# Residual additions for two tiles at a time, and three weight splits moved into the gated linear attention's score sets

## The reference

```python
def second_block(x, norm_gains, ...):
    h = x.astype(jnp.float32)
    for layer in range(DEPTH_2):
        g = norm_gains[layer]
        y = rms_norm_2(h, g[0])
        y = sb_gla_mixer(y, ...) if layer % 2 == 0 else s5_mixer(y, ...)
        h = h + rms_norm_2(y, g[1])
        y = swiglu_ffn(rms_norm_2(h, g[2]), w_ffn_in[layer], w_ffn_out[layer])
        h = h + rms_norm_2(y, g[3])

def sb_gla_mixer(h, ...):
...
    o_gla = gla_chunked(q, k, v, log_a)            # gated linear attention, 8 heads
    o_gla = o_gla * lax.rsqrt(jnp.mean(o_gla * o_gla, axis=-1, keepdims=True) + NORM_EPS)
    o_gla = merge_heads(o_gla) * gla_norm_gain * jax.nn.silu(g_r)
    return jnp.concatenate([o_sb, o_gla], axis=-1) @ w_out
```

## Time and profile before

| | |
|---|---|
| median of 3 runs | 3559.05 us (3557.74 to 3559.19) |
| the profiled execution: its own time | 3562.0 us |
| its span | 3560.2 us |
| TensorE busy | 3471.8 us (98%) |
| VectorE busy | 2306.5 us (65%) |
| ScalarE busy | 1785.4 us (50%) |
| GpSimd busy | 490.5 us (14%) |

### The profile page before, as it was taken

One profiled execution on the slowest core, in us unless ns is written; L12 is line 12 of the kernel. 1 busy time (PEld: TensorE's weight loads), 2 busy tenths in 40 slices (PEclk: granted clock), 3 DMA queues, 4 the chain that ended last, 5 costly groups with the idle time before them and its releaser, 6 DMA issues.

```text
span 3560.2 us, 62732 instructions
## 1 busy us (share of the span) xinstructions
PE 3471.8 (98%) x21888; PEld 3027.7 (85%) x21888; DVE 2306.5 (65%) x3460; ACT 1785.4 (50%) x2735; POOL 490.5 (14%) x538
## 2 busy tenths in 40 slices
PE   9998999999999999999999999999699999999998
PEld 7886888888888888888888888887588888888887
DVE  5688565555555766675766677779755665565566
ACT  5477454545454554554555444444354554454453
POOL 0001410111114100123100001105012000000005
PEclk9999999999999999999999999999899999999999
DMA  6561545555555555443456556666235455555555
GB/s 212 170 188 56 189 152 193 183 192 185 190 187 189 170 188 174 162 154 127 150 193 196 186 188 195 203 224 227 58 118 186 148 192 190 186 187 192 184 188 189
DMA packets 190643, 626.70 MB, mean 176 GB/s; under 512 B 26822, under 2 KB 40200, under 8 KB 190360
## 3 DMA queue, kind: packets, MB, share of 16 engines
q1 hardware_dynamic: 179948, 612.48, 52.8%
q10 hardware_dynamic: 10572, 12.56, 1.2%
HBM read 620.52 MB, written 3.15 MB: 175 GB/s over the span
## 4 chain that ended last, share of the span: by engine, by line
PE 88%; DVE 7%; ACT 2%; DMA 1%; issue 1%; POOL 0%; SPq 0%; ACTq 0%; DVEq 0%; POOLq 0%
PE bank L1901 53%; PE bank L1904 28%; PE m L1924 1%; DVE w_lo L1045 1%; PE m L1914 1%; PE m L1926 1%; DVE prod L1713 1%; DMA w_raw<-stream 1%; DVE y L1072 0%; DVE st L1718 0%; DVE st L1716 0%; DVE w_lo L1049 0%; ACT w_hi L465 0%; DVE res L1078 0%; PE m L2394 0%
## 5 line engine op out<-in xcount | busy, mean ns | idle before, releaser
L1045 DVE TENSOR_TENSOR w_lo<-w_raw,w_hi 128x1024 fp32r<-128x1024 f32 x1086 | 1336.3, 1253 | 773.1 <-ACT w_hi L465 766.4
L1901 PE MATMUL bank<-act,w_hi 128*128 128x512 f32 x6016 | 1511.6, 393 | 3.7 <-DVE w_lo L1045 1.7
L465 ACT ACTIVATE w_hi<-w_raw 128x1024 fp32r<-128x1024 f32 x1090 | 1128.9, 1054 | 404.5 <-PE bank L1904 358.2
L1901 PEld LDWEIGHTS bank<-act,w_hi 128*128 128x128 f32 x6016 | 1082.5, 189 | 203.7 <-DVE w_lo L1045 4.4
L1904 PEld LDWEIGHTS bank<-act,w_lo 128*128 128x128 f32 x6016 | 820.8, 191 | 58.7
L1904 PE MATMUL bank<-act,w_lo 128*128 128x256 f32 x6016 | 838.9, 282 | 0.0
L1901 PE MATMUL bank<-ffn,w_hi 128*128 128x512 f32 x2432 | 613.6, 393 | 2.2 <-DVE w_lo L1049 1.8
L474 ACT ACTIVATE low<-bank 128x256 f32<-128x256 f32 x542 | 207.4, 383 | 749.7 <-PE bank L1904 748.7
L1901 PEld LDWEIGHTS bank<-ffn,w_hi 128*128 128x128 f32 x2432 | 436.5, 189 | 81.0 <-DVE w_lo L1049 3.2
L1904 PEld LDWEIGHTS bank<-ffn,w_lo 128*128 128x128 f32 x2432 | 334.0, 190 | 25.1
L1053 DVE TENSOR_TENSOR ev<-bank,low 128x256 f32<-128x256 f32 x468 | 197.9, 423 | 240.5 <-ACT low L474 236.9
(11 more groups left out here) (419 smaller groups left out, 2268.6 us busy)
## 6 DMA issues: line engine op xcount, KB each, us to landing
w_raw<-stream SPq DMA_DIRECT2D x1148, 512.0 KB, 3.4
b_part<-s_bt ACTq DMA_DIRECT2D x16, 256.0 KB
pow_b<-powers ACTq DMA_DIRECT2D x16, 256.0 KB
bias<-toeplitz SPq DMA_DIRECT2D x4, 512.0 KB, 8.7
out<-res SPq DMA_DIRECT2D x3, 512.0 KB, 2.8
res<-x_t SPq DMA_DIRECT2D x2, 512.0 KB, 8.8
res<-x_t ACTq DMA_DIRECT2D x2, 512.0 KB, 11.0
bias<-toeplitz SPq DMA_DIRECT2D x4, 256.0 KB, 11.8
```

The source lines that it names most:

```text
L465: a(w_hi[:, q, :], w_raw[:, q, :], ACT.Copy).then_inc(hi_ready, 1)
L1045: e.tensor_tensor(w_lo[:, q, :], w_raw[:, q, :], w_hi[:, q, :].bitcast(F32), ALU.subtract).then_inc(lo_ready, 1)
L1901: mm(bank[w][:, 0:2 * n], w_hi[:, q, wt], x(h * hk + k, 0, 2 * n), start=(h == 0 and k == 0), stop=False)
```

## The change

Two parts. In `add_residual` two tiles are added in one operation of 512 columns; the scale runs two tiles ahead, the add of a pair waits for both scales, and the low parts of the pair before follow behind it, two in a row. In the second mixer, the splits of halves 1 and 2 of `out2`'s first step are taken out of the last step of `in2` and, with that of half 3, put at part 4 of the first three head pairs (`it` = 4, 9, 14); the filling of `row_of` goes to `it == 4`.

```diff
@@ add_residual
             scale(0)
-            for k in range(DT):
-                if k + 1 < DT:
-                    scale(k + 1)
-                v.wait_ge(y_scaled, base + k + 1)
-                e.tensor_tensor(res[:, k, :], res[:, k, :], y[:, k, :], ALU.add).then_inc(res_added, 1)
+            scale(1)
+            for k in range(0, DT, 2):
+                if k + 2 < DT:
+                    scale(k + 2)
+                v.wait_ge(y_scaled, base + k + 2)
+                e.tensor_tensor(res[:, k:k + 2, :], res[:, k:k + 2, :], y[:, k:k + 2, :], ALU.add).then_inc(res_added, 2)
+                if k + 3 < DT:
+                    scale(k + 3)
                 if low_part and k >= 2:
                     low_part(k - 2)
+                    low_part(k - 1)
                 if between:
                     between(k)
+                    between(k + 1)
             if low_part:
                 low_part(DT - 2)
                 low_part(DT - 1)
@@ VectorE, second mixer
-            run_phase(v, "in2", lo, scaled_z, behind=sb_behind, skip=1, quiet=8, lone=lone_z)
+            
+            def in2_low(i, q):
+                if not (isinstance(i, int) and i == PH["out2"][0] and q):
+                    lo(i, q)
+            run_phase(v, "in2", in2_low, scaled_z, behind=sb_behind, skip=1, quiet=8, lone=lone_z)
             v.wait_ge(sem("masks_loaded"), 16)
-
-            e.tensor_copy(row_of[:, :, :], ident[0:2, 0:2].unsqueeze(2).to_broadcast([2, 2, P])).then_inc(sem("row_of"), 1)
...
-                if it == 14:
-                    lo(PH["out2"][0], 3)
+                if it == 4:
+                    e.tensor_copy(row_of[:, :, :], ident[0:2, 0:2].unsqueeze(2).to_broadcast([2, 2, P])).then_inc(sem("row_of"), 1)
+                if part == 4 and t < 3:
+                    lo(PH["out2"][0], t + 1)
```

## The result

The changed kernel takes 3566.09 us (median of 12 runs, 3562.99 to 3569.49), the kernel before 3559.12 (12 runs beside it, 3557.15 to 3562.98). The ratio is 1.0019 with an interval of 1.0011 to 1.0026: slower by 7.0 us, where +6.45 and 3565.5 were forecast. It lies just inside the bound of 0.2%.

A forecast was written before the change was run, and what follows sets the result against it. The prediction took TensorE, busy 98% of the span, as the bound, VectorE mattering only where TensorE waits. Part one +3.45 and part two +3.0 made +6.45 us on the median 3559.05: 3565.5, range 3561.0 to 3568.5.

The forecast's parts named there:

- The prices: VectorE instruction times at the stage entries: a double add 0.60 us instead of 0.68 for two single adds.
- The feed-forward entries: MLP and both feed-forwards: TensorE's first tile 0.96 us later, 0.9 more per entry, +2.7 for three.
- The gate's entry: Gated projection: ScalarE waits 0.33 us longer for the ninth add, the fourth weight split 0.15 more; +0.5.
- The S5 entry: Entry to the S5 stage: the first square follows three scales and a double add, so TensorE starts later; +0.65 us.
- The end: End of the program, VectorE on the path: eight pairs give back 0.6 us, net -0.4; the two last stores cost nothing.
- The first select and the first split: Gated linear attention: select starts 3.0 us earlier, fillers leave 0.7, copy and split before set 5 use it up; -0.1.
- The second split: Gated linear attention, ahead of set 10's selects, VectorE on the path: all of it added, +1.5 us.
- The clock: Set 12 in the gated linear attention: TensorE falls to half clock behind the longer wait; +1.6 us.
- VectorE as the bound: Rival at the entries: VectorE sets the pace, so grouping's 0.6 us per entry comes back; 3554.9 us, chance 0.10.
- the dear double add: Rival: a double add takes the 0.68 us of two and saves nothing; 3566.1 us, chance 0.05.
- The clock staying up: Rival: no clock fall behind set 12's longer wait, so 1.6 us less; 3563.9 us, chance 0.28.
- Falls at the entries: Rival: the clock also falls at feed-forward entries; 3567.1 us with one fall, 3570.3 with three; chance 0.17.

The follow-up runs named there:

- run 7: Kernel before with each low part one tile behind its addition instead of two, at the feed-forward and gate entries, additions single: 3557.97 us, ratio 0.9996.
- run 4: The change's moved splits and copy with single additions, but the second split behind set 7's selects, against the kernel before: 3559.59 us, ratio 1.0001.
- run 8: Kernel before with double additions in the last stage alone and the last two stores made one: 3558.54 us, ratio 0.9997.
- run 10: Splits of run 5, feed-forward low parts of run 7, end of run 8, and 8 filler matmuls instead of 24 ahead of set 2: 3554.50 us.
- run 6: Run 2 with 12 filler matmuls set into each of TensorE's waits before sets 12 and 17: 3560.29 us, ratio 1.0002 against the kernel before.
- run 11: The kernel before, unchanged, run again for a second trace: 3558.41 us, ratio 0.9997.
- run 1: The double additions alone, splits and copy as in the kernel before: 3564.85 us against 3559.5, ratio 1.0014.
- run 3: Kernel before with each stage's first four tiles added singly and the other twelve in pairs, splits as before: 3563.51 us, ratio 1.0012.
- run 5: Run 4 with the third split moved behind the loop, ahead of the last reciprocal: 3556.85 us against 3559.96 for the kernel before, ratio 0.9990.
- run 2: The moved splits and copy of the change alone, additions single as in the kernel before: 3563.26 us, ratio 1.0011.

## Why the prediction was right

- **The prices.** Double add 0.61 from start to start, taken as 0.60. Right.
- **The feed-forward entries.** First tile 0.99 later (0.96 forecast), each entry +0.87 (0.9). "What VectorE saves later has nobody waiting for it" holds: nothing came back. Run 7 shows the cause with the sign turned. The sentence on breaking instructions up in the Trainium skill, "Perfetto Trace Analysis", section "Optimizing Scalar/DVE Operations", says that where an engine isn't saturated but makes others wait, smaller instructions may let work finish sooner. The traces agree: on an engine at 65%, working in pairs made TensorE's idle time ahead of its first tile grow from 0.56 to 1.55. The size of the instruction is the small part of it: by the prediction's own prices 0.78 of the 0.96 are the two scales that the pairs draw ahead of the first low part, and 0.18 the adds.
- **The gate's entry.** +0.59, taken as 0.5. ScalarE's work behind the ninth add starts 0.38 later (1186.01, before 1185.64, from reciprocals 0.01 apart), forecast 0.33; the other 0.21 come behind it, where 0.15 was given to the fourth split. **The S5 entry.** From the first scale to the first square's sum +0.66, taken as 0.65; the other 1.0 in after is a fall of the clock that began ahead of the entry and that run 4 has with single additions.
- **The end.** Sized wrong: -0.05 instead of -0.4. The step that failed is "each is small, and I cost that at nothing": the issue of a store, 0.4, which used to hide beside the last addition, now stands behind it (run 8).
- **The first select and the first split.** Place right, sum too high: -0.1 was forecast, and from the reciprocal at 1286.68 to the first one inside the attention it is -0.88 (307.70 to 306.82). Of this 0.55 is the copy's price: I took 0.75 for it from its old place, and in the new one it takes 0.20 (1585.51 to 1585.71). The select before it was also done some 0.3 sooner than I had it. Run 10 shows that the fillers were what held set 2, as forecast.
- **The second split.** +1.5 forecast, 1.56 measured (run 6); run 4 removes it by moving that one split.
- **The clock.** +1.6 forecast behind set 12, 1.46 in the trace of after, and run 6 removes it with fillers. What I had wrong is that this was told as one certain event at one place. Falls come and go between executions of one kernel: after has one behind 2.19 us and none behind nearly the same wait at set 17, and the kernel before fell behind that wait in its first trace and not in its second (run 11). The two traces that were compared have two falls in the attention before and one after, so in them the attention is even 1.02 shorter with the change.
- **The sum.** Without falls the traces give 3 x 0.87 + 0.59 + 0.66 - 0.05 = +3.8 for part one and -0.88 + 1.56 = +0.7 for part two, together +4.5, where the forecast without its clock term was 4.85. The forecast then added one fall, 1.6. The measured +7.0 (by the interval, 3.9 to 9.3) leaves 2.5 for the clock, and the mean clock of the executions (run 6) gives about two more falls, 3.2 by that estimate. So the mechanism holds, but 6.45 came as near as it did by luck: the end was 0.35 too hopeful, the first select 0.8 too dear, and the clock was taken as one fall where it is nearer to two. Where the second one comes is open: the S5 entry of after has one, behind set 17's wait it has none, and one trace for each kernel can't give frequencies by place.
- **The rivals.** VectorE as the bound is out (run 7, and no gain behind the first tiles); the dear double add is out (0.61). The clock staying up holds in some executions at one of the two waits. Falls at the entries: none at the three feed-forward entries of after, in spite of 1.55 us without work. The falls near S5's entry (after, runs 1 and 4) and near ffn1's (runs 1, 3, 5 and 10) all began ahead of the first scale of their stage, from 0.4 us before to 1.0 behind its reciprocal, so the longer idle time ahead of the first tile did not bring them. The three kernels with double additions at the entries (after, runs 1 and 3) have five of the eight starred entries in the table; whether that is chance is not shown.

## What to carry to other kernels

Where VectorE feeds a saturated TensorE, count what stands ahead of the first output that the other engine waits for, and not the instructions in all: working in pairs moved that output 1.0 us back and saved nothing that anyone waited for, and taking one step out ahead of it gave 0.73 an entry. Put loose work where the engine waits anyway (the split behind set 7 or ahead of the last reciprocal), not between two sets of a hand-over that is already the path. To judge a change of 0.1% in a kernel whose clock falls by chance, compare stretches between the same two instructions and count the falls in each; how often a kernel falls is read from the mean clock of many executions.

## What was not expected of the hardware

- The length of a wait does not decide whether the clock falls behind it: the traces of all kernels hold eleven waits of TensorE of 2.12 to 2.19 us ahead of set 12 or 17. In five the set behind ran at half clock for most or all of it (1.72 to 2.08 us instead of 1.16: before, after at set 12, twice in run 2, run 8), in six it did not (after at set 17, runs 1, 3, 4, 7, 11), though in run 3 the fall began right behind that set, at 1615.7. Each fall inside the attention cost 1.4 to 1.6 us. With the waits filled, run 6's executions are back at the mean clock of the kernel before.
- The copy of 2x256 took 0.75 of VectorE in its old place and 0.20 in the new one. In the old place GpSimd was at work (its first tile from 1579.38, the copy from 1579.53), in the new one it began behind the copy (1585.69 and 1585.51). The splits show that it is not always VectorE that pays. The one at 1597.90 began 0.17 behind GpSimd and took 1.56 instead of 1.14. The one at 1585.71 stands beside a GpSimd tile as well and took 1.15; there it was GpSimd's instruction that grew, to 1.82 from 0.73 (1585.98 in before):

```profile
1585.69 1.82 POOL L1792 TENSOR_TENSOR act<-z,act 128x256 fp32r<-128x256 f32 x1 [3.64 <-ACT act L894]
1597.73 2.39 POOL L1872 TENSOR_TENSOR z<-z 128x256 f32<-128x256 f32 x2 [1.89 <-DVE z L1673]
```

  The Trainium skill, "SBUF — State Buffer", section "Who interferes with whom", names the pair of ports that the two engines share as an exclusive lock. These numbers fit two engines that wait for each other; no run here took GpSimd away, so it is argued and not shown.
- An operation directly behind the one whose output it reads started 0.57 after it instead of 0.39 (run 3).
